# Splitting the experts' up projection into high and low parts, with thinner gathers and six weight places

## The chip, the cores and the metric

One NeuronCore of a Trainium2 chip runs the whole program in one launch. The metric is the device time of that core in microseconds, the median of several runs; a profiled execution gives the trace. Engines: TensorE (PE), VectorE (DVE), ScalarE (ACT), GpSimd (POOL) and SyncE (SP), which only issues transfers.

## The reference, cut to what matters

Two blocks run one after the other on 512 rows of 1024 channels in fp32. The change touches only the last part of the second block, the routed experts:

```python
# 512 tokens, 32 experts, each token goes to 2 experts: 1024 (token, expert) pairs
hf = rmsnorm(x, ffn_norm_g)                     # 512 x 1024
# group top-1 of 4, then top-2 of the 8 experts of that group, gates by softmax
for each expert e, its tokens t (on average 32):
    gt, up = split(hf[t] @ w_gu[e])             # 1024 -> 512, halves of 256
    y = (silu(gt) * up) @ w_down[e]             # 256 -> 1024
    out[t] += gate[t, e] * y
x = x + out
return rmsnorm(x, final_norm_g)
```

Each expert has 2 MB of w_gu and 1 MB of w_down, so 96 MB in all are read once.

## The kernel before, in words

Every engine has its own program, written out by hand (`mo_pe`, `mo_act`, `mo_dve`, `mo_pool`, SyncE's `sp_program`), and named semaphore counts order them: `did(name, key)` counts, `at(name, key)` is what a wait needs. An engine runs its program strictly in the written order.

Before the experts' part come dense layers. They already use a split form: ScalarE copies a weight unit of 128x1024 into WH rounded to fp32r, VectorE writes WL = raw - WH, the activations lie as HH and HL (or R_op, R_ffn), and TensorE adds three fp32r products (high x high, low x high, high x low). In the experts' part of the kernel before, all matmuls are plain fp32.

The experts' part starts with the routing: logits, one-hot choices, ranks, and a matmul that makes for each expert a list of up to 128 places, each with a token number (`mo.idx`), a destination row (`mo.dix`, where an unused place gets a number beyond the last row) and a gate (`mo.gsl`). The normalised rows are stored to DRAM (`hdram`). Line 2388 writes `mo.idx`; an unused place has 0 there, so a gather reads row 0 for it.

Then the loop over 32 experts x (lines 2184 to 2210 for TensorE). POOL gathers 128 rows of 4 KB into one of three places `mo.Xg` and, when done, scatters the results to `ydram` from `mo.Y`. TensorE, in order: the up matmuls of x (8 row tiles, held operand `mo.XT` 128x128, streamed operand 512 weights); 8 transposes of the rows of x+1 (`turned`); the down matmuls of x-1 (`down`, 4 matmuls); for x from 2 to 9 also 4 transposes of the residual; 2 transposes of the hidden rows of x. ScalarE does the sigmoid, half of the copies out of PSUM of the transposed rows, half of the output with the gate, and the hidden rows' copy; VectorE does the products with the sigmoid (two steps of 128x256), the other half of the rows, and the other half of the output. Eight PSUM banks are handed out in a fixed turn (`Turn`).

SyncE loads weights in the order of the list XW: up chunk 0, up chunk 1 of x, down chunk of x-1, 1 MB each, into a ring of nine places (NEXP = 9, `RX`). A place is loaded again when the matmuls that read it nine transfers earlier are done (line 2108). The first nine are issued once the merge before is done; then the rows are stored to DRAM; then the rest.

If an expert has more than 128 rows a guarded part (`ov_...`) handles the rest; it doesn't run in the profile shown.

Of the kernel before, what the change touches and what calls it, by code (L numbers as in the profile page):

```python
# [6 lines left out]
F32 = mybir.dt.float32  # L7
# [9 lines left out]
S = 512  # L17
D = 1024
# [3 lines left out]
NUNIT = 3  # L22
NEXP = 9
NMOE = 20976
BIG = 1.0e30
# [5 lines left out]
for _name, _w in (("ident", 128), ("ones", 128), ("ones64", 128), ("rot64", 128), ("rot32", 128),  # L31
                  ("cd", 128), ("sd", 128), ("tmask", 896), ("causal", 512), ("strict", 128),
                  ("incl64", 64), ("strict64", 64), ("hexp", 128), ("invf64", 1), ("invf32", 1), ("iota", 32), ("io128", 128), ("tok", 4), ("tok2", 4), ("tok3", 4)):
    CO[_name] = (_n, _w)
    _n += _w
# [184 lines left out]
def build(nc, I, out):  # L220
    ctx = ExitStack()
    with ctx:
# [36 lines left out]
        A_sec = phase("second", NA)[0]  # L259
        fast.close()  # L260
        with ExitStack() as st:
            A_moe, RX = sb(st, "A_moe", NMOE), sb(st, "ring_moe", NEXP * SLOT)
# [1794 lines left out]
        NB = 3  # L2057
        ar = Arena(A_moe, 0, 14336)
        mo.htok = t3(ar.take(4 * D), 4)
        mo.Xg = [ar.take(D) for _ in range(NB)]  # L2060
        mo.XT = [t3(ar.take(D), 8) for _ in range(2)]
        mo.sg, mo.hu, mo.hT = ([ar.take(256) for _ in range(2)] for _ in range(3))
        mo.Y = [ar.take(D) for _ in range(NB)]
        ar = Arena(A_moe, 14336, NMOE)
        mo.H = t3(ar.take(8 * S), 8)
# [11 lines left out]
        mo.idx, mo.dix, mo.gsl = ar.take(32).bitcast(U32), ar.take(32).bitcast(U32), ar.take(32)  # L2077
        ov = Mix()
        ov.sel, ov.pos, ov.g, ov.r = ar.take(32), ar.take(4), ar.take(4), ar.take(4)
# [4 lines left out]
        mo.P = [mo.Y[0][:, 0:S], mo.Y[0][:, S:2 * S]]  # L2084
        gu_rows = I["w_gu"].rearrange("e j p n -> (e j p) n")
# [18 lines left out]
        def sp_expert(e, n):  # L2104
            kind, x, j = XW[n]
            if n >= NEXP:
                k0, x0, j0 = XW[n - NEXP]
                e.wait_ge(*at("mo_pe", k0, x0))
            src = I["w_gu"][x, j] if kind == "up" else I["w_dn"][x]
            e.dma(RX[:, n % NEXP * SLOT:(n % NEXP + 1) * SLOT], src).then_inc(*sent(f"x{n % NEXP}", *XW[n]))  # L2110

        MO = tuple(range(8))

        def mo_pe(e):
# [70 lines left out]
            for x in range(32):  # L2185
                b = bank()
                e.wait_ge(*at("mo_act", "xt", x))
                e.wait_ge(*at("mo_dve", "xt", x))
                for j in range(2):
                    w, loaded = xslot("up", x, j)  # L2190
                    e.wait_ge(*loaded)
                    for kt in range(4):
                        t = e.mm(b, mo.XT[x % 2][:, j * 4 + kt, :], w[:, kt * S:(kt + 1) * S], j + kt == 0, j + kt == 4)
                t.then_inc(*did("mo_pe", "up", x))
                if x < 31:
                    turned(x + 1)
# [12 lines left out]
                t.then_inc(*did("mo_pe", "ht", x))  # L2209
# [3 lines left out]
        def mo_act(e):  # L2213
# [25 lines left out]
            turn.next()  # L2239

            def turned(x):
                n, b = turn.next()
                turn.next()
                e.wait_ge(*at("mo_pe", "xt", x, 0))
                if x >= 2:
                    e.wait_ge(*at("mo_pe", "up", x - 2))
                e.act(mo.XT[x % 2][:, 0:4, :], t3(b, 4), ACT.Copy).then_inc(*read("mo_act", turn, n))
                mark("mo_act", "xt", x)

            def down(x):  # L2250
# [8 lines left out]
                mark("mo_act", "y", x)  # L2259

            turned(0)
            for x in range(32):
                n, b = turn.next()
                e.wait_ge(*at("mo_pe", "up", x))
                if x >= 2:
                    e.wait_ge(*at("mo_dve", "hu", x - 2))
                e.act(mo.sg[x % 2], b[:, 0:256], ACT.Sigmoid).then_inc(*did("mo_act", "sg", x))
                if x < 31:
                    turned(x + 1)
                if x:  # L2270
                    down(x - 1)
# [46 lines left out]
        def mo_dve(e):  # L2318
# [43 lines left out]
            for i, (oh, own) in enumerate(((mo.oh1, "tok2"), (mo.oh2, "tok3"))):  # L2362
                e.tt(mo.R[i][:, :, :, 0], oh, bcast(c("tok"), 2, 32), MUL)
                e.tt(mo.R[i][:, :, :, 1], oh, bcast(c(own), 2, 32), MUL)
# [22 lines left out]
            e.wait_ge(*at("mo_pe", "list"))  # L2387
            e.cp(mo.idx, bv[:, :, 0]).then_inc(*did("mo_dve", "idx"))
            e.ts(mo.dix, bv[:, :, 1], 4096.0, None, ADD)
# [12 lines left out]
            step(e.cp(mo.flag, mo.uc[:, 31:32]), "flag")  # L2402

            def turned(x):
                turn.next()
                n, b = turn.next()
                e.wait_ge(*at("mo_pe", "xt", x, 1))
                if x >= 2:
                    e.wait_ge(*at("mo_pe", "up", x - 2))
                e.cp(mo.XT[x % 2][:, 4:8, :], t3(b, 4)).then_inc(*read("mo_dve", turn, n))  # L2410
                mark("mo_dve", "xt", x)

            def down(x):
# [52 lines left out]
        def ov_dve(e0):  # L2466
# [3 lines left out]
            with e0.raw.If(many > 0):  # L2470
# [6 lines left out]
                for j in range(7):  # L2477
# [28 lines left out]
                    for f2 in range(2):  # L2506
                        t = e.cp(mo.XT[0][:, f2 * 4:f2 * 4 + 4, :], t3(bk(f2), 4))
                    t.then_inc(*did("ov_dve", j, "xt"))
# [11 lines left out]
        def ov_pe(e0):  # L2520
            many = over(e0)
            with e0.raw.If(many > 0):
                e = inner(e0)
                for j in range(7):
# [10 lines left out]
                    for kt in range(8):  # L2535
                        t = e.mm(bk(2), mo.XT[0][:, kt, :], RX[:, kt * S:(kt + 1) * S], kt == 0, kt == 7)
                    t.then_inc(*did("ov_pe", j, "gu"))
# [249 lines left out]
def constants():  # L2787
# [41 lines left out]
    put("io128", i[None])  # L2829
    put("tok", i[:, None] + 128 * np.arange(4)[None])  # L2830
    put("tok2", 2 * (i[:, None] + 128 * np.arange(4)[None]) - 4096)
    put("tok3", 2 * (i[:, None] + 128 * np.arange(4)[None]) - 4095)
# [85 lines left out]
```

## Time and profile before

| | us |
|---|---|
| median of 3 runs | 2578.49 (2576.56 to 2578.68) |
| the profiled execution, its own time | 2576.27 |
| its span in the trace | 2574.5 |
| mean granted TensorE clock | 0.934 |
| PE busy | 2380.1 (92%) |
| DVE / ACT / POOL busy | 1150.3 / 757.3 / 192.4 |
| first up matmul of expert 0, last matmul of the loop | 2172.7, 2544.5 |

The page divides the span in 40 slices of 64 us; the digits are tenths of busy time, or of the full clock. The experts' loop takes slices 34 to 39. A group of instructions shows the line of a helper in the code, since each kind of operation has one: L122 matmul, L125 transpose, L129 activation, L135 tensor_tensor, L139 tensor_scalar, L146 copy, L167 transfer, L170 gather, L174 scatter. So groups are told apart by tile. A_moe is the memory of the experts' part, ring_moe the ring of weights. A duration of a matmul in the trace is longer than its step, since matmuls overlap: start to start is the price.

### The profile page before, as it was taken

How to read it: one execution, taken by the hardware profiler on the slowest of the kernel's cores; microseconds unless marked ns; L12 is line 12 of the kernel's file. 1: busy time of each engine (PE TensorE's matmuls, PEld its weight loads, DVE VectorE, ACT ScalarE, POOL GpSimd, SP SyncE). 2: the span in 40 equal slices, each digit the busy share in tenths (PEclk: the TensorE clock that was granted, in tenths of full speed). 3: DMA queues.
4: the chain of work that ended last, by engine and by line, in shares of the span. 5: the costliest groups of instructions: out<-in, count | busy, mean ns of one | idle time of the engine just before them, and what ended most of it. 6: DMA issues, size and time to landing. Idle time of an engine off the chain costs nothing.

```text
span 2574.5 us, 32881 instructions
## 1 busy us (share of the span) xinstructions
PE 2380.1 (92%) x14232; PEld 1722.6 (67%) x14232; DVE 1150.3 (45%) x1771; ACT 757.3 (29%) x1171; POOL 192.4 (7%) x167
## 2 busy tenths in 40 slices
PE   6997799999999987899999998999699998999995
PEld 5884478888888854688888766888344466544442
DVE  6646555435445465555254586333332332111123
ACT  5332543213333324532123332122222122221112
POOL 1112010000001130000000200000000010111110
PEclk9998899999999997999999998999875896999997
DMA  4211012222222110022222221112310043889983
GB/s 159 71 66 49 1 50 98 95 92 93 96 98 68 64 50 17 33 98 98 98 94 92 85 86 59 68 59 72 113 49 1 33 186 128 307 326 340 342 326 145
DMA packets 52420, 283.78 MB, mean 110 GB/s; under 512 B 9136, under 2 KB 9264, under 8 KB 23088
## 3 DMA queue, kind: packets, MB, share of 16 engines
q1 hardware_dynamic: 42048, 257.72, 27.7%
q0 software_dynamic: 9216, 20.99, 2.2%
q8 instruction: 114, 1.87, 0.3%
q10 hardware_dynamic: 1008, 2.92, 0.3%
q14 instruction: 34, 0.28, 0.0%
HBM read 267.44 MB, written 26.74 MB: 114 GB/s over the span
## 4 chain that ended last, share of the span: by engine, by line
PE 84%; DVE 8%; ACT 3%; issue 2%; POOL 1%; DMA 1%; SPq 0%; POOLq 0%; ACTq 0%; DVEq 0%
PE psum L122 81%; PE psum L125 3%; POOL A_mix L135 1%; DVE A_second L135 1%; DVE A_mix L135 1%; ACT A_mix L129 1%; DVE A_second L143 1%; DVE WL L135 1%; DVE A_mix L149 1%; DMA raw<-in_w_in 0%; ACT not_lins L132 0%; DVE A_second L149 0%; DVE A_moe L135 0%; POOL RS L135 0%; ACT HH L129 0%
## 5 line engine op out<-in xcount | busy, mean ns | idle before, releaser
L135 DVE TENSOR_TENSOR WL<-raw,WH 128x1024 fp32r<-128x1024 f32 x236 | 294.8, 1251 | 397.5 <-ACT WH L129 397.4
L129 ACT ACTIVATE WH<-raw 128x1024 fp32r<-128x1024 f32 x236 | 248.4, 1054 | 442.2 <-PE psum L122 431.1
L122 PE MATMUL psum<-ring_moe,A_moe 128*128 128x512 f32 x768 | 343.1, 597 | 1.8 <-DVE A_moe L146 1.1
L122 PE MATMUL psum<-HH,WH 128*128 128x512 f32 x736 | 303.8, 413 | 37.3 <-DVE HL L143 19.2
L122 PE MATMUL psum<-R_op,WH 128*128 128x512 f32 x1024 | 316.1, 390 | 0.0
L122 PE MATMUL psum<-R_ffn,WH 128*128 128x512 f32 x1024 | 315.2, 389 | 0.0
L122 PE MATMUL psum<-HL,WH 128*128 128x512 f32 x736 | 291.2, 396 | 0.0
L122 PE MATMUL psum<-HH,WL 128*128 128x512 f32 x736 | 290.7, 395 | 0.0
L122 PE MATMUL psum<-A_mix 64*128 64x64 f32 (+5 forms) x1984 | 189.1, 328 | 75.4 <-DVE small L161 38.7
L122 PEld LDWEIGHTS psum<-ring_moe,A_moe 128*128 128x128 f32 x768 | 142.1, 192 | 158.0 <-issue 158.0
L122 PE MATMUL psum<-A_second 64*64 64x64 f32 (+3 forms) x3736 | 222.7, 250 | 7.8 <-DVE A_second L135 4.6
L122 PEld LDWEIGHTS psum<-R_op,WH 128*128 128x128 f32 x1024 | 192.2, 188 | 40.8 <-issue 1.0
L122 PEld LDWEIGHTS psum<-R_ffn,WH 128*128 128x128 f32 x1024 | 192.2, 188 | 39.9
L122 PEld LDWEIGHTS psum<-A_mix 64*128 64x128 f32 (+2 forms) x1984 | 132.1, 183 | 117.2 <-DVE small L161 45.4
L122 PEld LDWEIGHTS psum<-A_second 64*64 64x64 f32 (+3 forms) x3736 | 151.8, 144 | 74.3 <-issue 65.5
L122 PE MATMUL psum<-R_op,WL 128*128 128x512 f32 x512 | 199.2, 389 | 0.0
L122 PE MATMUL psum<-R_ffn,WL 128*128 128x512 f32 x512 | 199.2, 389 | 0.0
L122 PEld LDWEIGHTS psum<-HH,WH 128*128 128x128 f32 x736 | 141.0, 192 | 79.3 <-issue 33.5
L122 PEld LDWEIGHTS psum<-HL,WH 128*128 128x128 f32 x736 | 141.2, 192 | 30.1 <-issue 2.9
L122 PEld LDWEIGHTS psum<-HH,WL 128*128 128x128 f32 x736 | 140.8, 191 | 30.7
L129 ACT ACTIVATE A_moe<-psum 128x256 f32<-128x256 f32 (+1 forms) x104 | 47.6, 466 | 265.2 <-PE psum L122 209.4
L135 DVE TENSOR_TENSOR A_moe<-psum,A_moe 128x256 f32<-128x256 f32 (+1 forms) x34 | 14.1, 416 | 224.5 <-ACT A_moe L129 224.5
(191 smaller groups left out, 2691.2 us busy)
## 6 DMA issues: line engine op xcount, KB each, us to landing
ring_moe<-in_w_gu SPq DMA_DIRECT2D x64, 1024.0 KB, 7.1
raw<-in_w_in SPq DMA_DIRECT2D x42, 1024.0 KB, 4.8
raw<-in_w_up SPq DMA_DIRECT2D x32, 1024.0 KB, 4.8
raw<-in_w_down SPq DMA_DIRECT2D x32, 1024.0 KB, 4.8
ring_moe<-in_w_dn SPq DMA_DIRECT2D x32, 1024.0 KB, 7.4
raw<-in_w_out SPq DMA_DIRECT2D x12, 1024.0 KB, 4.8
kept<-A_second SPq DMA_DIRECT2D x22, 256.0 KB, 2.1
A_second<-kept SPq DMA_DIRECT2D x22, 256.0 KB, 5.7
```

Of the source, the lines that this page charges most:

```text
L122: return self.raw.matmul(o, l, r, start=start, stop=stop)
L125: return self.raw.matmul(o, i, ident, is_transpose=True, start=True, stop=True)
L129: return self.raw.activation(o, i, f, scale=scale)
L135: return self.raw.tensor_tensor(o, a, b, op)
L143: return self.raw.scalar_tensor_tensor(o, a, s, b, op0, op1)
L149: return self.raw.reciprocal(o, a)
```

## The change

It does four things. (1) The up matmuls become three fp32r products: new tiles XH, XL (rows) and a ring of four units WH, WL (NSPLIT = 4) of 128x1024, that is a quarter of an expert's w_gu each. ScalarE writes the high parts (`high(u)`), VectorE the low parts (`low(u)`), in their loops where the diff puts them. ScalarE now copies both halves of the turned rows as XH, and VectorE subtracts both as XL. (2) `mo.idx` of an unused place becomes 4096, past the last row, so that the gather leaves it out (its place in Xg keeps what was there; no result of it is used). (3) NEXP 9 becomes 6; a place of an up chunk is free when VectorE has made the low part of its second unit, that of a down chunk when the down matmuls are done. (4) The tiles are laid out anew in the same total memory: XH, XL, WH, WL share what HH, HL, WH, WL of the dense layers used.

```diff
-NEXP = 9
-NMOE = 20976
+NEXP = 6
+NSPLIT = 4
+NMOE = 27120
@@ sp_expert
-                e.wait_ge(*at("mo_pe", k0, x0))
+                e.wait_ge(*(at("mo_dve", "w", 4 * x0 + 2 * j0 + 1) if k0 == "up" else at("mo_pe", "dn", x0)))
@@ mo_pe, loop over x
-                e.wait_ge(*at("mo_act", "xt", x))
                 e.wait_ge(*at("mo_dve", "xt", x))
-                for j in range(2):
-                    w, loaded = xslot("up", x, j)
-                    e.wait_ge(*loaded)
-                    for kt in range(4):
-                        t = e.mm(b, mo.XT[x % 2][:, j * 4 + kt, :], w[:, kt * S:(kt + 1) * S], j + kt == 0, j + kt == 4)
-                t.then_inc(*did("mo_pe", "up", x))
+                for i in range(4):
+                    u = 4 * x + i
+                    e.wait_ge(*at("mo_dve", "w", u))
+                    wh, wl = mo.WH[u % NSPLIT], mo.WL[u % NSPLIT]
+                    for k in range(2):
+                        kt, cs = 2 * i + k, slice(k * S, (k + 1) * S)
+                        xh, xl = mo.XH[x % 2][:, kt, :], mo.XL[x % 2][:, kt, :]
+                        e.mm(b, xh, wh[:, cs], kt == 0, False)
+                        e.mm(b, xl, wh[:, cs], False, False)
+                        t = e.mm(b, xh, wl[:, cs], False, kt == 7)
+                    t.then_inc(*did("mo_pe", "w", u))
+                mark("mo_pe", "up", x)
@@ mo_act
+            def high(u):
+                if u < 128:
+                    w, loaded = split_of(u)
+                    e.wait_ge(*loaded)
+                    if u >= NSPLIT:
+                        e.wait_ge(*at("mo_pe", "w", u - NSPLIT))
+                    e.act(mo.WH[u % NSPLIT], w, ACT.Copy).then_inc(*did("mo_act", "w", u))
@@ mo_act, turned(x)
+                for f2 in range(2):
+                    n, b = turn.next()
+                    e.wait_ge(*at("mo_pe", "xt", x, f2))
+                    if x >= 2:
+                        e.wait_ge(*at("mo_pe", "up", x - 2))
+                    e.act(mo.XH[x % 2][:, 4 * f2:4 * f2 + 4, :], t3(b, 4), ACT.Copy).then_inc(*did("mo_act", "xt", x, f2))
@@ mo_act, loop over x
+            for u in range(4):
+                high(u)
             turned(0)
             for x in range(32):
                 n, b = turn.next()
+                for i in range(3):
+                    high(4 * x + 4 + i)
                 e.wait_ge(*at("mo_pe", "up", x))
                 ... sigmoid
                 if x < 31:
                     turned(x + 1)
+                high(4 * x + 7)
                 if x:
                     down(x - 1)
@@ mo_dve
-            e.cp(mo.idx, bv[:, :, 0]).then_inc(*did("mo_dve", "idx"))
+            e.ts(mo.idx, bv[:, :, 0], 4096.0, None, ADD).then_inc(*did("mo_dve", "idx"))
+            def low(u):
+                if u < 128:
+                    w, _ = split_of(u)
+                    e.wait_ge(*at("mo_act", "w", u))
+                    e.tt(mo.WL[u % NSPLIT], w, mo.WH[u % NSPLIT].bitcast(F32), SUB).then_inc(*did("mo_dve", "w", u))
@@ mo_dve, loop over x
+            for u in range(4):
+                low(u)
             turned(0)
             for x in range(32):
                 n, b = turn.next()
+                for i in range(2):
+                    low(4 * x + 4 + i)
                 e.wait_ge(*at("mo_act", "sg", x))
                 ... two products
                 if x < 31:
                     turned(x + 1)
+                for i in range(2):
+                    low(4 * x + 6 + i)
                 if x:
                     down(x - 1)
```

VectorE's `turned(x)` becomes two subtractions out of PSUM (bank minus XH) in the same manner. The constant `tok4` (token number less 4096) takes the place of `tok` in the lists.

## Rows read from the trace of the kernel before

**Rows 1.** Loop by window: busy us of PE, PEld, DVE, ACT, POOL; clock; DMA share; GB/s.
```profile
2230.00:2502.87 272.87, 272.87 (x827) 134.05 (x826) 51.25 (x93) 50.75 (x100) 48.73 (x48) 1.00 0.90 332
```
**Rows 2.** Order of time in the loop: start us, us, engine, line, operation, count.
```profile
2343.32 1.04 PE L125 MATMUL psum<-C,A_moe 128*128 128x128 f32 x8
2344.19 3.60 PE L122 MATMUL psum<-ring_moe,A_moe 128*128 128x512 f32 x8
2347.63 0.38 PE L125 MATMUL psum<-C,A_moe 128*128 128x128 f32 x2
2347.84 7.03 PE L122 MATMUL psum<-ring_moe,A_moe 128*128 128x512 f32 x16
2354.71 1.04 PE L125 MATMUL psum<-C,A_moe 128*128 128x128 f32 x8
...
2343.93 0.42 DVE L135 TENSOR_TENSOR A_moe<-psum,A_moe 128x256 f32<-128x256 f32 x1 [6.75 <-ACT A_moe L129]
```
**Rows 3.** Order of time, dense fp32r matmuls: alone, then between other work.
```profile
2119.77 0.39 PE L122 MATMUL psum<-HL,WH 128*128 128x512 f32 x1
2120.00 0.19 PEld L122 LDWEIGHTS psum<-HH,WH 128*128 128x128 f32 x1
...
2125.21 0.39 PE L122 MATMUL psum<-HL,WH 128*128 128x512 f32 x1
...
1490.48 0.39 PE L122 MATMUL psum<-HH,WL 128*128 128x512 f32 x1
1490.80 1.99 PE L122 MATMUL psum<-A_second 64*128 64x512 f32 x8
1492.71 0.50 PE L122 MATMUL psum<-HH,WH 128*128 128x512 f32 x1
...
1498.31 0.39 PE L122 MATMUL psum<-HH,WH 128*128 128x512 f32 x1
```
**Rows 4.** Groups (busy us, mean ns, idle before): whole span; loop; feed-forward (last row).
```profile
L135 DVE TENSOR_TENSOR WL<-raw,WH 128x1024 fp32r<-128x1024 f32 x236 | 294.8, 1251 | 397.5 <-ACT WH L129 397.4
L129 ACT ACTIVATE WH<-raw 128x1024 fp32r<-128x1024 f32 x236 | 248.4, 1054 | 442.2 <-PE psum L122 431.1
...
L170 POOL DMA_INDIRECT A_moe<-h_rows,A_moe x24 | 24.5, 1020 | 7.3 <-issue 7.3
L129 ACT ACTIVATE A_moe<-psum 128x256 f32<-128x256 f32 x47 | 18.0, 384 | 170.0 <-PE psum L122 147.5 <-PE psum L125 22.4
L139 DVE TENSOR_SCALAR A_moe<-psum,A_moe 128x512 f32<-128x512 f32 x24 | 18.0, 751 | 57.9 <-PE psum L122 57.9
L129 ACT ACTIVATE A_moe<-psum 128x512 f32<-128x512 f32 x29 | 17.3, 597 | 10.0 <-PE psum L125 8.8
L129 ACT ACTIVATE A_moe<-psum,A_moe 128x512 f32<-128x512 f32 x24 | 16.5, 687 | 37.4 <-PE psum L122 37.4
...
L135 DVE TENSOR_TENSOR relu<-psum,RS 128x512 f32<-128x512 f32 x5 | 3.5, 691 | 6.9 <-PE psum L122 6.9
```
**Rows 5.** Order of time from before the first to the second up.
```profile
2171.42 1.28 ACT L129 ACT_TABLE_LOAD   x1
2172.67 10.02 PE L122 MATMUL psum<-ring_moe,A_moe 128*128 128x512 f32 x16 [1.05 <-DVE A_moe L146]
2184.73 0.67 PE L122 MATMUL psum<-ring_moe,A_moe 128*128 128x512 f32 x1 [0.21 <-issue]
```
**Rows 6.** Landing of the loop's weight loads; the first loads' burst by stage; DMA queue.
```profile
DMA to landing us min/median/max: 4.7/7.2/10.2
2118.00:2123.00 5.00, 5.00 (x24) 4.14 (x23) 0.39 (x1) 1.25 (x2) 1.61 (x2) 1.00 1.01 419
q0 software_dynamic: 9216, 20.99, 2.2%
```
**Rows 7.** Windows, columns as rows 1: attention; start of the experts.
```profile
1950.00:1975.00 25.00, 25.00 (x71) 12.20 (x71) 5.54 (x26) 7.22 (x20) 0.00 (x0) 0.50 0.00 0
2175.00:2180.00 5.00, 5.00 (x9) 1.97 (x8) 0.00 (x0) 0.00 (x0) 0.00 (x0) 0.65 0.15 61
```

More of the change, by code:

```diff
@@ L260, in build @@
         fast.close()
+        with ExitStack() as st:
+            R_moe = sb(st, "R_moe", (4 + 2 * NSPLIT) * D, F32R)
         with ExitStack() as st:
@@ L2057, in build @@
         NB = 3
[L2058 to L2061, printed above, removed]
+        rm = Arena(R_moe, 0, (4 + 2 * NSPLIT) * D)
+        mo.XH, mo.XL = ([t3(rm.take(D), 8) for _ in range(2)] for _ in range(2))
+        mo.WH, mo.WL = ([rm.take(UNIT) for _ in range(NSPLIT)] for _ in range(2))
+        ar = Arena(A_moe, rm.lo, 14336)
         mo.sg, mo.hu, mo.hT = ([ar.take(256) for _ in range(2)] for _ in range(3))
-        mo.Y = [ar.take(D) for _ in range(NB)]
-        ar = Arena(A_moe, 14336, NMOE)
+        ar = Arena(A_moe, 20976, NMOE)
+        mo.htok = t3(A_moe[:, 20976:20976 + 4 * D], 4)
+        mo.Xg, mo.Y = ([ar.take(D) for _ in range(NB)] for _ in range(2))
+        ar = Arena(A_moe, 14336, 20976)
         mo.H = t3(ar.take(8 * S), 8)
@@ L2078, in build @@
         ov = Mix()
+        ov.XT = t3(mo.Xg[1], 8)
         ov.sel, ov.pos, ov.g, ov.r = ar.take(32), ar.take(4), ar.take(4), ar.take(4)
@@ L2083, in build @@
         mo.ss, mo.rr = ar.take(4), ar.take(4)
-        mo.P = [mo.Y[0][:, 0:S], mo.Y[0][:, S:2 * S]]
+        mo.P = [mo.Y[1][:, 0:S], mo.Y[1][:, S:2 * S]]
         gu_rows = I["w_gu"].rearrange("e j p n -> (e j p) n")
@@ L2107, in sp_expert, with split_of @@
                 k0, x0, j0 = XW[n - NEXP]
-                e.wait_ge(*at("mo_pe", k0, x0))
+                e.wait_ge(*(at("mo_dve", "w", 4 * x0 + 2 * j0 + 1) if k0 == "up" else at("mo_pe", "dn", x0)))
             src = I["w_gu"][x, j] if kind == "up" else I["w_dn"][x]
             e.dma(RX[:, n % NEXP * SLOT:(n % NEXP + 1) * SLOT], src).then_inc(*sent(f"x{n % NEXP}", *XW[n]))
+        def split_of(u):
+            w, loaded = xslot("up", u // 4, u % 4 // 2)
+            return w[:, u % 2 * UNIT:(u % 2 + 1) * UNIT], loaded
         MO = tuple(range(8))
@@ L2239, in mo_act @@
             turn.next()
-            def turned(x):
[L2242 to L2248, printed above, removed]
+            def high(u):
[5 more added lines that the diff above has]
+                    e.act(mo.WH[u % NSPLIT], w, ACT.Copy).then_inc(*did("mo_act", "w", u))
+            def turned(x):
+                for f2 in range(2):
[4 more added lines that the diff above has]
+                    e.act(mo.XH[x % 2][:, 4 * f2:4 * f2 + 4, :], t3(b, 4), ACT.Copy).then_inc(*did("mo_act", "xt", x, f2))
             def down(x):
@@ L2362, in mo_dve @@
             for i, (oh, own) in enumerate(((mo.oh1, "tok2"), (mo.oh2, "tok3"))):
-                e.tt(mo.R[i][:, :, :, 0], oh, bcast(c("tok"), 2, 32), MUL)
+                e.tt(mo.R[i][:, :, :, 0], oh, bcast(c("tok4"), 2, 32), MUL)
                 e.tt(mo.R[i][:, :, :, 1], oh, bcast(c(own), 2, 32), MUL)
@@ L2402, in mo_dve @@
             step(e.cp(mo.flag, mo.uc[:, 31:32]), "flag")
-            def turned(x):
[L2405 to L2410, printed above, removed]
+            def low(u):
[3 more added lines that the diff above has]
+                    e.tt(mo.WL[u % NSPLIT], w, mo.WH[u % NSPLIT].bitcast(F32), SUB).then_inc(*did("mo_dve", "w", u))
+            def turned(x):
+                for f2 in range(2):
+                    n, b = turn.next()
+                    e.wait_ge(*at("mo_act", "xt", x, f2))
+                    e.tt(mo.XL[x % 2][:, 4 * f2:4 * f2 + 4, :], t3(b, 4), mo.XH[x % 2][:, 4 * f2:4 * f2 + 4, :].bitcast(F32),
+                         SUB).then_inc(*read("mo_dve", turn, n))
                 mark("mo_dve", "xt", x)
@@ L2506, in ov_dve @@
                     for f2 in range(2):
-                        t = e.cp(mo.XT[0][:, f2 * 4:f2 * 4 + 4, :], t3(bk(f2), 4))
+                        t = e.cp(ov.XT[:, f2 * 4:f2 * 4 + 4, :], t3(bk(f2), 4))
                     t.then_inc(*did("ov_dve", j, "xt"))
@@ L2535, in ov_pe @@
                     for kt in range(8):
-                        t = e.mm(bk(2), mo.XT[0][:, kt, :], RX[:, kt * S:(kt + 1) * S], kt == 0, kt == 7)
+                        t = e.mm(bk(2), ov.XT[:, kt, :], RX[:, kt * S:(kt + 1) * S], kt == 0, kt == 7)
                     t.then_inc(*did("ov_pe", j, "gu"))
@@ L2830, in constants @@
     put("tok", i[:, None] + 128 * np.arange(4)[None])
+    put("tok4", i[:, None] + 128 * np.arange(4)[None] - 4096)
     put("tok2", 2 * (i[:, None] + 128 * np.arange(4)[None]) - 4096)
```

2 lines of the change are left out of this document (1 added, 1 removed).

## Prediction

> **What bounds the kernel now.** I read the page's table of 40 slices first: from about 2170 us to the end TensorE, the clock and the DMA are all high at once, and only this stretch, the experts' loop, is changed. The busy times by stage come next [rows 1]: over 273 us TensorE is busy for the whole window at full clock (1.00 is the 2.4 GHz level), with the DMA at 0.90 of its time, VectorE at 51 us and ScalarE at 51 us. So TensorE has no gap to give back; only less TensorE work can shorten the loop, until another resource is late. The order of time on TensorE [rows 2] gives one expert: 8 transposes of gathered rows 2343.32 to 2344.19 (0.87), 4 down matmuls in 8 halves to 2347.63 (3.44), 2 transposes of the hidden rows to 2347.84 (0.21), 8 up matmuls in 16 halves to 2354.71 (6.87). Period: 2354.71 - 2343.32 = **11.39 us**. An fp32 matmul here runs as two halves of 0.43 us each.
>
> **The up matmuls.** Removed: 8 fp32 matmuls, 6.87 us per expert. Added: 24 in fp32r (three products for each of 8 row tiles). Their shape, 128x128 held and 128x512 streamed, is that of the dense layers. [rows 3] bracket their price: from 2119.77 to 2125.21 lie 24 steps, 5.44 us, so 0.227 each where nothing but fp32r runs; the 24 steps from 1492.71 to 1498.31, just after other work, take 5.60, and leaving fp32r takes 0.32 instead of 0.23 (1490.48 to 1490.80), 0.09 more. The new loop has both seams in each expert, so I take the second: 5.60 + 0.09 = 5.69, saving 1.18; the other end is 5.44, saving 1.43. New period **10.21** (9.96 without seams). Held operands are now rows and streamed ones weights, the other way round than in those rows; the shapes are the same, so I price this swap at nothing, and the rival "no overlap of loads" covers its failure.
>
> **The splitting, beside TensorE.** Per expert ScalarE gets 4 copies of 128x1024 (1.05 each) and one more 128x512 copy (0.60); VectorE gets 4 subtractions of 128x1024 (1.25) and two of 128x512 from PSUM (0.69) in place of one copy [rows 4]. Whole load: ScalarE 4x1.05 + 2x0.60 + 0.38 + 0.69 + 0.38 = 6.85; VectorE 4x1.25 + 2x0.69 + 2x0.42 [rows 2] + 0.75 = 7.97. Both are under 10.21, but order decides. I lay one period out, t = 0 at the first up matmul of expert x. The first product with the sigmoid starts 0.61 us after the next transposes begin, 0.38 of it the sigmoid [rows 2, 4]; I give 0.2 of the rest to the hand-over from TensorE and 0.03 to that between the others. A place of WH is free after each six matmuls, at 1.40, 2.80, 4.20. ScalarE: high parts of the next expert's units at 1.45, 2.85 and 4.25 to 5.3, sigmoid 5.9 to 6.3, XH 6.35 to 7.55, last high part to 8.6, output half 8.6 to 9.3, hidden copy at 10.4. VectorE: low parts 2.5 to 3.75 and 3.9 to 5.15, hidden rows 6.3 to 7.2, XL 7.2 to 8.6, low parts to 11.1, output half to 11.85. TensorE: transposes 5.69 to 6.56, down 6.56 to 10.0, next up at 10.21. It wants XL, ready at 8.6 (slack 1.6); its third low part at 13.0, ready at 9.85 (slack 3.1). The added waits thus find their events long past. What is queued behind them: behind ScalarE's wait for a WH place the sigmoid (0.6 us of room); behind VectorE's wait for the sigmoid the XL parts and the last two low parts. PSUM places are re-used after eight turns, six or seven of them in one period, as before. If this cover is gone, every us past 1.6 in the chain up, sigmoid, hidden rows, XL is paid in full, 31 times.
>
> **Six weight places.** A weight place is now freed by VectorE's low part and not by the last up matmul; but SyncE issues in order, so the next two up chunks stand behind the wait of a down chunk, which is free at -0.2. Issues: down and first up chunk at -0.2, second up chunk at 0.9 (after the low part that ends at 11.1 of the period before). Wanted: first up chunk at 11.7, second at 14.5, down chunk at 16.8; so they have 11.8, 13.6 and 17.0 us. Landings in the loop took 4.7 to 10.2, median 7.2 [rows 6]. Fewer places therefore cost nothing, with 1.6 us left above the longest landing.
>
> **Gathers.** A gather brings 128 rows of 4 KB (0.52 MB); the 32 scatters together write the 1024 valid ones (4.2 of the 21.0 MB of the software queue [rows 6]), so 32 gathers move 16.8 MB and would move 4.2. Per expert 3.15 + 0.52 + 0.13 = 3.80 MB becomes 3.41. On a critical path that is worth nothing while TensorE paces; it pays for the faster loop. The loop's 332 GB/s at a share of 0.90 means 369 GB/s, so 9.2 us per expert; the burst of first loads ran at 419 GB/s [rows 6], so 8.1. Both are below 10.21. POOL's 1.02 us for each gather [rows 4] I leave, though it could shrink with the rows; POOL waits most of the loop anyway (49 of 273 us busy, [rows 1]).
>
> By the Trainium skill (SBUF — State Buffer, "A bandwidth-pool intuition that's wrong"), a core gets about 358 GB/s from HBM; the burst row is above that, so the trace disagrees. By that figure the transfers would need 9.5 us per expert, and the sum would be the same with 0.7 us of room.
>
> The new subtractions read two SBUF operands while POOL writes descriptors. No row shows the two together in the loop; bounds are 0 and the whole 1.02 us twice per expert on VectorE: 7.97 + 2.03 = 10.0, still under 10.21, and a gather issued two experts ahead has over 10 us. I take 0.
>
> The Trainium skill (SBUF — State Buffer, "SBUF: two separate sides") has VectorE instructions with two SBUF inputs and GpSimd instructions that read SBUF exclude one another for their whole length; that speaks against this change, and the bound just given holds what it could cost.
>
> **Start and end.** Before: the first rows are turned at half clock, the first up starts at 2172.67 and takes 9.86 us since the clock is 0.50, and 0.65 on average from 2175 to 2180: full for the last 0.3 of these 5 us, so from 2178.5; the second starts at 2184.73 [rows 5, 7]. After: four low parts (5 us) go ahead of the first row parts on VectorE, behind the routing, whose last steps run while the gather is under way. I take them as hidden behind the gather: XL starts at 2171.7 (the first XH is there by 2171.4, where the table load starts) and ends at 2173.1, so +0.4; if nothing hid them, it would be up to +5. Half clock until 2178.5 does 5.4/0.454 = 12 matmuls, the other 12 end near 2181.3. But ScalarE's table load for the sigmoid (1.28 us, now hidden at 2171.42) will come behind the third high part, 2181.0 to 2182.3; so sigmoid 2182.7, hidden rows 2183.6, XL 2185.0. The second up starts at 2185.0 rather than 2184.7: **+0.3 us**. Bounds 0 to +8: the four low parts unhidden, or half clock through the whole first expert (3 us more). The end (last down, reload of results, norm) has no changed step.
>
> **Sum.** 31 x 1.18 = 36.6, less 0.3 = 36.3 us. The profiled execution took 2576.3 us, 1.8 more than its 2574.5 span and 2.2 less than the median of 2578.5; the span should become 2538.2, and the median **2542.2 us**. Without seams: 31 x 1.43 - 0.3 = 44.0, or 2534.5.
>
> **Rivals.**
> A, TensorE paces (my forecast), period 9.96 to 10.5: 2534 to 2551. For it: all slack above. Chance 0.77.
> B, hand-overs or landings are late by some tenths up to 1 us per expert: the SyncE issues come in a burst of three, so landings could rise over 11.8 us, or the XL chain could be 2 us longer than laid out. At 0.7 us per expert: 2542 + 31x0.7 = 2564 (range 2551 to 2573). For: landings of 10.2 already with nine places. Against: less traffic. Chance 0.14.
> C, no overlap of weight loads with the stream: 0.19 (load) + 0.23 (step, [rows 3]) = 0.42 per matmul, 24 are 10.1 us, 3.2 more than now; the place is the up part, it decides from 0.286 per matmul (6.87/24), and the time is 2578.5 + 31x3.2 = 2678, slower. Against: in [rows 3] each load starts with the previous matmul. Chance 0.02.
> D, the clock stays low. [rows 7] has a stretch in which TensorE is busy for all 25 us and the clock is still 0.50, and the new start has two gaps of over 1 us. Each expert at half clock costs 10.2 more; it decides at 3.6 experts, and through the whole loop it gives 2542 + 31x10.2 = 2858, slower. Against: dense fp32r windows stand at 1.00 throughout [rows 3], and so did the loop's fp32 [rows 1]. Chance 0.03.
> E, the edit saves matmul time but the waits give just that much back (within 5 us of 2578.5): 0.04.
> The Trainium skill (TensorE: Matmul & The Clock Gate, "HAM oscillation") has thin tiles of 128 rows drop to the low clock when TensorE waits for loads between them; it would add to D, with D's time, and the loop's row at 1.00 speaks against it.
>
> **How the numbers follow.** Range: A in full and B up to 2558: 2533 to 2558, which leaves out half of B and C, D, E, and a little of A's fast side: some 0.18. A change of 0.2% is 5.2 us, about what can be told here. Faster: A and B, 0.91, plus the small-stall side of E and D, 0.01: 0.92; same 0.04; slower 0.04.
>
> **What would show it.** Period on TensorE of 10.2 with no idle between transposes and up; 24 matmuls in 5.4 to 5.7; clock 1.00 from the second expert; DMA share about 0.80 to 0.90 at 330 to 340 GB/s; XL ending 1.5 us before the next up; software queue 8.4 MB. Idle on TensorE released by VectorE's XL or WL would show B; a weight load not under the matmul before it, C; PEclk under 1 after 2190 us, D.

## The result

The changed kernel takes **2533.9 us** (median of 4 runs, 2533.3 to 2537.0) against 2577.5 of the kernel before on the same chips: 43.6 us less, ratio 0.983 (95% interval 0.982 to 0.985). The forecast was 2542.2 within 2533 to 2558. The span of the profiled execution is 2531.1 us against 2574.5.

The loop by window, columns as in [rows 1]: TensorE is still busy for the whole window at full clock; VectorE's share went from 0.19 to 0.74, ScalarE's from 0.19 to 0.67, and the DMA moves about as many GB/s as before, with fewer bytes per expert in a shorter period.

```profile
2230.00:2470.00 240.00, 240.00 (x1019) 168.84 (x1018) 176.50 (x215) 160.56 (x220) 62.32 (x47) 1.00 0.88 338
```

TensorE's order of time in the loop of the changed kernel, which answers to [rows 2]:

```profile
2333.35 1.04 PE L126 MATMUL psum<-C,A_moe 128*128 128x128 f32 x8
2334.22 3.60 PE L123 MATMUL psum<-ring_moe,A_moe 128*128 128x512 f32 x8
2337.66 0.38 PE L126 MATMUL psum<-C,A_moe 128*128 128x128 f32 x2
2337.80 5.73 PE L123 MATMUL psum<-R_moe 128*128 128x512 f32 x24
2343.36 1.04 PE L126 MATMUL psum<-C,A_moe 128*128 128x128 f32 x8
```

From start to start: rows' transposes 0.87, down part 3.44, hidden rows' transposes 0.14 (0.21 before), up part 5.56 (6.87 before). Period 2343.36 - 2333.35 = **10.01 us** against 11.39: 1.38 less, for two reasons of 1.31 and 0.07.

What runs beside it, in the same period (order of time; the number in brackets is the idle time before, with its releaser):

```profile
2333.55 0.38 ACT L130 ACTIVATE A_moe<-psum 128x256 f32<-128x256 f32 x1 [0.25 <-PE psum L123]
2333.99 1.08 ACT L130 ACTIVATE R_moe<-psum 128x512 fp32r<-128x512 f32 x2
2334.76 1.28 DVE L136 TENSOR_TENSOR R_moe<-psum,R_moe 128x512 fp32r<-128x512 f32 x2
2335.96 2.35 DVE L136 TENSOR_TENSOR R_moe<-ring_moe,R_moe 128x1024 fp32r<-128x1024 f32 x2
...
2340.63 2.53 DVE L136 TENSOR_TENSOR R_moe<-ring_moe,R_moe 128x1024 fp32r<-128x1024 f32 x2 [1.65 <-ACT R_moe L130]
2341.15 1.60 POOL L171 DMA_INDIRECT A_moe<-h_rows,A_moe  x1 [0.30 <-issue]
```

XL ends at 2334.76 + 1.28 = 2336.04, and the next up part starts at 2337.80: 1.76 us of slack. The gather on GpSimd takes 1.60 here, and 1.02 in [rows 4].

The time that weight loads of the loop take from issue to landing (min, median, max us), which answers to [rows 6], and the software queue on the page:

```profile
DMA to landing us min/median/max: 4.7/8.0/13.2
...
DMA packets 52424, 271.26 MB, mean 107 GB/s; under 512 B 12208, under 2 KB 12336, under 8 KB 23088
q0 software_dynamic: 9216, 8.42, 1.0%
```

The start of the experts' part, answering to [rows 5]; TensorE, and the table load on ScalarE:

```profile
2167.26 1.97 PE L126 MATMUL psum<-C,A_moe 128*128 128x128 f32 x8 [4.50 <-DMA A_moe<-h_rows,A_moe]
2171.44 7.54 PE L123 MATMUL psum<-R_moe 128*128 128x512 f32 x24 [2.21 <-DVE R_moe L136]
2178.80 1.28 ACT L130 ACT_TABLE_LOAD   x1
2178.82 1.04 PE L126 MATMUL psum<-C,A_moe 128*128 128x128 f32 x8
2181.44 0.44 PE L126 MATMUL psum<-C,A_moe 128*128 128x128 f32 x2 [1.58 <-DVE A_moe L136]
2182.64 7.11 PE L123 MATMUL psum<-R_moe 128*128 128x512 f32 x24 [0.76 <-DVE R_moe L136]
```

**Where the 43.4 us of span went.** The second expert's up part starts 2.1 us earlier (2184.73 to 2182.64); from there to the start of the last expert's up part the kernel before needs 345.5 us and the changed one 305.4 (2182.64 to 2488.00), 40.1 less; from there to the last down part 11.25 and 9.93, 1.3 less; the end is equal within 0.1. The 40.1 are 30 periods of 1.38 less 1.3 us for the second expert, whose up part took 6.95 us because the clock was not yet full. Of the 2.1 us at the start 1.8 lie ahead of the first changed step of TensorE, ScalarE or VectorE: the transposes of the normalised rows start at 2147.62 against 2149.39. From there to the issue of the first gather 0.6 is lost (2163.93 against 2165.12), while TensorE makes the lists at a lower clock (3.70 us against 3.11). From that issue to the first rows' transposes 1.2 is won (3.33 us against 4.53), and from these to the second up part 0.3 is lost.

### The profile page after: what moved, and what is told of

Read it like the earlier page. It is cut to its first block, busy times and chain, and to the rows that moved or that the text cites. A ratio compares the mean times of both kernels' runs of the same rounds, so it can differ in the third digit from the quotient of the medians.

```text
span 2531.1 us, 33743 instructions
## 1 busy us (share of the span) xinstructions
PE 2336.0 (92%) x14488; PEld 1770.0 (70%) x14488; DVE 1317.5 (52%) x1931; ACT 904.2 (36%) x1331; POOL 212.6 (8%) x167
## 2 busy tenths in 40 slices
DMA packets 52424, 271.26 MB, mean 107 GB/s; under 512 B 12208, under 2 KB 12336, under 8 KB 23088
## 3 DMA queue, kind: packets, MB, share of 16 engines
q0 software_dynamic: 9216, 8.42, 1.0%
## 4 chain that ended last, share of the span: by engine, by line
PE 84%; DVE 8%; ACT 3%; issue 2%; POOL 1%; DMA 1%; SPq 0%; ACTq 0%; POOLq 0%; DVEq 0%
PE psum L123 81%; PE psum L126 3%; POOL A_mix L136 1%; DVE A_second L136 1%; DVE A_mix L136 1%; ACT A_mix L130 1%; DVE A_second L144 1%; DVE WL L136 1%; DVE A_mix L150 1%; ACT not_lins L133 0%; DMA raw<-in_w_in 0%; DVE A_moe L136 0%; DVE A_second L150 0%; POOL RS L136 0%; ACT HH L130 0%
## 5 line engine op out<-in xcount | busy, mean ns | idle before, releaser
L123 PE MATMUL psum<-R_moe 128*128 128x512 f32 x768 | 186.7, 400 | 3.0 <-DVE R_moe L136 3.0
L136 DVE TENSOR_TENSOR R_moe<-ring_moe,R_moe 128x1024 fp32r<-128x1024 f32 x128 | 153.5, 1221 | 60.8 <-ACT R_moe L130 58.3
L123 PEld LDWEIGHTS psum<-R_moe 128*128 128x128 f32 x768 | 144.3, 191 | 32.9 <-issue 2.6
L130 ACT ACTIVATE R_moe<-ring_moe 128x1024 fp32r<-128x1024 f32 x128 | 135.5, 1062 | 55.7 <-PE psum L123 55.7
```

What stands on the lines that cost most here:

```text
L123: return self.raw.matmul(o, l, r, start=start, stop=stop)
L130: return self.raw.activation(o, i, f, scale=scale)
L136: return self.raw.tensor_tensor(o, a, b, op)
```

## The experiments

The theory: TensorE paces both loops; the gain is its matmul time and nothing else; six places and thin gathers are only room. The rivals are that the gain, or part of it, is relief of the transfers; or that the new work beside TensorE already costs something. Medians are held against the kernel before on the same chip (2575.6 to 2576.2), as ratios with their 95% interval; "above the changed kernel" means above its 2534 to 2535 us.

**Full gathers in the changed kernel.**

```diff
-                e.tt(mo.R[i][:, :, :, 0], oh, bcast(c("tok4"), 2, 32), MUL)
+                e.tt(mo.R[i][:, :, :, 0], oh, bcast(c("tok"), 2, 32), MUL)
-            e.ts(mo.idx, bv[:, :, 0], 4096.0, None, ADD).then_inc(*did("mo_dve", "idx"))
+            e.cp(mo.idx, bv[:, :, 0]).then_inc(*did("mo_dve", "idx"))
```

> The changed kernel with the full gathers back: an unused place reads row 0 again, 0.52 MB per expert and not 0.13. Theory (TensorE paces, 10.01 us per expert in the changed kernel's trace): the transfers need 3.80 MB per expert; at the burst's 419 GB/s that is 9.1 us, so nothing is lost: within 3 us of the changed kernel's 2534. Rival (the transfers would pace without the thin gathers): at 369 GB/s, the rate that the old loop implies, it is 10.3 us, 0.3 us per expert over TensorE's 10.01, so 2534 + 31 x 0.3 = 2543; if it is worse, idle time of TensorE before the first up matmul or before the splits shows it. A gather takes 1.72 us on GpSimd in the changed kernel and took 1.02 before: if the 1.72 stays here, the new VectorE work and not the left-out places lengthens it.

Measured: 2533.9 us, ratio 0.984 (0.983 to 0.986), so nothing lost. The same window of the loop:

```profile
2230.00:2470.00 240.00, 240.00 (x1019) 168.61 (x1018) 175.90 (x215) 160.52 (x220) 62.54 (x47) 1.00 0.97 377
```

The DMA stands at 0.97 of its time with 377 GB/s and TensorE still doesn't wait. The rate implied by [rows 1], 369 at a full share, was too low as a limit. So the thin gathers gave nothing of the 43.6 us that can be told from the noise, though they keep the DMA further from its limit. What they do change is the first landing. In the ten profiles with thin gathers the first rows' transposes start 3.2 to 3.5 us after the start of the first gather's instruction, and in the four with full ones 4.4 to 4.6. In the changed kernel XL then waits for the low parts, so that only 0.5 us of this reaches the first up part (7.51 us after that start, 8.04 with full gathers).

**Thin gathers alone in the kernel before** (the reverse edit).

> The kernel before with one part of the change alone: gathers leave out the unused places. Theory: TensorE paces at 11.39 us per expert with or without it, so no difference: 2577 within 2 us, and the DMA's busy share in the loop falls from 0.90 to about 0.80 (3.41 MB per 11.39 us, 300 GB/s). Rival (the gain came from relieved transfers): a good part of the 43.6 us appears here. A gather on GpSimd: 1.02 us if the VectorE splits are what lengthens it to 1.72, 1.7 if the left-out places do.

Measured: 2574.2 us, ratio 1.000 (0.999 to 1.001). Share 0.83 and 299 GB/s. The gathers on GpSimd in this kernel (min, median, max ns, count), their landing, and the same two lines of the changed kernel with full gathers:

```profile
L170 POOL DMA_INDIRECT A_moe<-h_rows,A_moe x25: 1017/1017/1024, 2199.6 to 2476.6; - x25
DMA to landing us min/median/max: 4.5/5.6/6.9
```

```profile
L171 POOL DMA_INDIRECT A_moe<-h_rows,A_moe x27: 1512/1591/2027, 2206.7 to 2470.7; - x27
DMA to landing us min/median/max: 8.8/10.0/12.2
```

Left-out places don't lengthen a gather's instruction (1.02 us in the first fence). In the changed kernel it takes 1.5 to 2.0 us, with full gathers too, and the traces show when: if it starts while VectorE runs a subtraction of two SBUF operands, it ends 2.12 us after that subtraction began, as if it waited for its end and then took its 1.02. In the changed kernel it starts 0.52 us into one and takes 1.60 (2340.63 and 2341.15 above), or 0.10 into one and takes 2.02. In the run with five places below it starts 0.34 into one and takes 1.78; the next gather there starts 0.23 us ahead of the subtraction and takes 1.02. One that starts with a subtraction (2165.44 and 2165.43 in the changed kernel) takes 1.00 as well. The two of the run with five places:

```profile
2335.67 1.78 POOL L171 DMA_INDIRECT A_moe<-h_rows,A_moe  x1 [0.30 <-issue]
2345.64 1.02 POOL L171 DMA_INDIRECT A_moe<-h_rows,A_moe  x1 [0.30 <-issue]
```

By the Trainium skill (SBUF — State Buffer, "SBUF: two separate sides") such an instruction and a GpSimd one that reads SBUF exclude each other, and whichever starts first keeps the other waiting for the whole instruction. These durations agree on the side of GpSimd alone: VectorE's subtractions take 1.22 us in the loop and 1.25 in the dense layers [rows 4], and the pair that starts behind the gather at 2345.64 takes 2.36 us, as pairs do elsewhere in that run.

**Six places alone in the kernel before.**

```diff
-NEXP = 9
+NEXP = 6
```

> The kernel before with six weight places in place of nine, nothing else. Theory: a load is still issued a whole period ahead, so nothing changes: 2577 within 2 us. An up chunk is issued when the up matmuls of two experts earlier end, and wanted 4.5 us plus one up part less than two periods later, over 11 us; landings took up to 10.2. Rival: with six places the fp32 loop waits for loads, by up to 1 us per expert, 2577 to 2608, and the shorter hold of a place by the splits is what makes six enough.

Measured: 2575.4 us, ratio 1.000 (0.999 to 1.001); landings 4.7 to 10.3, median 7.7. Fewer places cost nothing there.

**Half a dose: one chunk of two split.** The second chunk of each expert runs as four fp32 matmuls from rows copied in fp32; only half of the high and low parts are made.

```diff
-                for i in range(4):
+                for i in range(2):
...
+                w, loaded = xslot("up", x, 1)
+                e.wait_ge(*loaded)
+                for kt in range(4):
+                    t = e.mm(b, mo.XT[x % 2][:, kt, :], w[:, kt * S:(kt + 1) * S], False, kt == 3)
```

> The changed kernel with the split for one of the two up chunks of each expert alone; the other runs as four plain fp32 matmuls, as before. A half dose: if TensorE's matmul time is all of the gain, the up part takes 12 x 0.227 + 8 x 0.43 + 0.1 = 6.2 us in place of 5.56 (changed) and 6.87 (before), the period is 10.7, and the time lies in the middle: 2534 + 31 x 0.66 = 2554. Rival (the price is in changes between fp32r and fp32 work, 0.1 to 0.3 us each, which this version has once more): up to 6.5 us for the up part, 2563. Rival (the gain is of another kind, such as less traffic, which stays whole here): 2534.

Measured: 2551.7 us, ratio 0.991 (0.989 to 0.992). The period:

```profile
2340.00 1.04 PE L126 MATMUL psum<-C,A_moe 128*128 128x128 f32 x8
2340.87 3.60 PE L123 MATMUL psum<-ring_moe,A_moe 128*128 128x512 f32 x8
2344.30 0.38 PE L126 MATMUL psum<-C,A_moe 128*128 128x128 f32 x2
2344.44 3.02 PE L123 MATMUL psum<-R_moe 128*128 128x512 f32 x12
2347.30 3.59 PE L123 MATMUL psum<-ring_moe,A_moe 128*128 128x512 f32 x8
2350.73 1.04 PE L126 MATMUL psum<-C,A_moe 128*128 128x128 f32 x8
```

10.73 us, between 11.39 and 10.01, with 12 fp32r steps in 2.86 and 8 halves in 3.43. The full dose saved 1.38 per expert, the half 0.66: the loop's gain is the matmul time, and it grows in proportion. (The whole run saves more than half, 24.5 of 40.8 us on this chip, because its start is shorter too: from the first rows' transposes to the second up part its profile has 12.6 us, where the changed kernel has 15.4 and 15.9.) The price of a change between the two kinds is small: 2.86 - 12 x 0.227 = 0.14.

**2.3 us put into the chain to XL.** Four needless copies follow the sigmoid.

```diff
                 e.act(mo.sg[x % 2], b[:, 0:256], ACT.Sigmoid).then_inc(*did("mo_act", "sg", x))
+                if x < 31:
+                    for i in range(4):
+                        e.act(mo.scr, Xt[:, 0, :], ACT.Copy).then_inc(*did("mo_act", "dup", x, i))
+                        e.wait_ge(*last("mo_act"))
```

> The changed kernel with four needless copies of 128x512 on ScalarE right behind the sigmoid, per expert but the last, each waited for: about 4 x 0.64 = 2.6 us put into the chain up part, sigmoid, XH, XL, next up part. In the changed kernel's trace XL ends at 2336.04 and the next up part starts at 2337.80: slack 1.76. Theory (the chain has that slack and beyond it each us is paid in full): 2.6 - 1.8 = 0.8 us per expert, 31 x 0.8 = +25 us, 2559, with TensorE idle before the up part released by VectorE's XL. Rival 1 (the chain already paces): +2.6 per expert, 2614. Rival 2 (slack wider than it looks): no change, 2534.

Measured: 2555.2 us, ratio 0.992 (0.991 to 0.994), 21 us above the changed kernel. The wait that is new:

```profile
2337.68 1.29 DVE L136 TENSOR_TENSOR R_moe<-psum,R_moe 128x512 fp32r<-128x512 f32 x2 [2.25 <-ACT R_moe L130]
2338.25 0.38 PE L126 MATMUL psum<-C,A_moe 128*128 128x128 f32 x2
2339.03 5.77 PE L123 MATMUL psum<-R_moe 128*128 128x512 f32 x24 [0.40 <-DVE R_moe L136]
```

XL ends at 2338.97 and the up part starts 0.06 later. The period is 10.69 (transposes of the hidden rows at 2338.25 and 2348.94), 0.68 over 10.01; 31 x 0.68 = 21. XL came 2.3 us later after the sigmoid, of which 1.7 was slack. So the chain has the slack that the trace showed, and past it the time is paid in full.

**Two more subtractions on VectorE.**

```diff
+                    for i in range(1):
+                        e.tt(t3(mo.scr, 4), t3(b, 4), mo.XH[x % 2][:, 4 * f2:4 * f2 + 4, :].bitcast(F32), SUB).then_inc(*did("mo_dve", "dup", x, f2, i))
+                        e.wait_ge(*last("mo_dve"))
                     e.tt(mo.XL[x % 2][:, 4 * f2:4 * f2 + 4, :], ...
```

> The changed kernel with two needless subtractions of 128x512 out of PSUM on VectorE, one ahead of each XL part, each waited for: 2 x 0.74 = 1.5 us more work on VectorE in each expert and 1.5 us later XL. Theory: the slack of 1.76 covers the chain, and VectorE's own work of 7.6 + 1.5 = 9.1 us stays under the 10.01 us period, so 2534 within 3 us. Rival (VectorE, once its waits for ScalarE's high parts are counted, is as long as the period): up to +1.5 per expert, 2580.

Measured: 2536.1 us, ratio 0.985 (0.984 to 0.987). The loop's period stays 10.01 (up parts at 2340.95 and 2350.96); some 1.5 us come before each of the first two up parts, where XL is on the path (TensorE idle for 3.65 and 2.21 us there, in place of 2.21 and 0.76). VectorE is then busy 208 of 240 us and still doesn't pace.

**Five places.**

```diff
-NEXP = 6
+NEXP = 5
```

> The changed kernel with five weight places in place of six. It measures how much room the ring has. With six, loads are issued in a burst of three when a down chunk's place comes free (2337.86 to 2339.1 in the trace) and take up to 13.2 us (median 8.0); an up chunk is wanted about 11.5 us after its issue. With five a place is asked for again five transfers later: the first up chunk of x+2 waits for the second up chunk of x (its low part ends at the end of the period), the second for the down part before it, the down chunk for the first up chunk. Theory: each load is issued a third of a period later (3.3 us), so with 8 us to land and about 8 us left it comes in about on time: between 0 and 1 us lost per expert, 2534 to 2565, with idle time released by ring_moe's loads. Rival (six is already at the edge, as landings of 13 us suggest): over 2 us per expert, above 2596.

Measured: 2537.2 us, ratio 0.985 (0.983 to 0.986), 2 to 3 us above the changed kernel, which isn't clear of the noise since the intervals overlap; TensorE is busy 239.2 of 240 us. Now loads are late for their first reader:

```profile
ACT R_moe L130 <- DMA ring_moe<-in_w_gu: 42.8, 36, 3.5
```

42.8 us of ScalarE's time in 36 waits, the longest 3.5, nearly all of it taken up by the slack of the splits. So with five the loads begin to be late, and six has room.

**Without the third product.** It is left out of the computation.

```diff
                         e.mm(b, xh, wh[:, cs], kt == 0, False)
-                        e.mm(b, xl, wh[:, cs], False, False)
-                        t = e.mm(b, xh, wl[:, cs], False, kt == 7)
+                        t = e.mm(b, xl, wh[:, cs], False, kt == 7)
```

> The changed kernel without the third product (high rows x low weights), which is left out of the computation: 8 matmuls fewer per expert, all else as it is, the splits included. It asks what is late next behind TensorE. TensorE alone: 10.01 - 8 x 0.227 = 8.2 us per expert, 31 x 1.8 = 56 us less, 2478. VectorE's own work is 4 x 1.22 + 2 x 0.68 + 2 x 0.42 + 0.74 = 7.8 us and ScalarE's 6.9, both near it. Transfers: 3.41 MB need 8.1 us at 419 GB/s, 9.2 us at 369. Theory: the transfers or the order of VectorE's work take over at about 9.0 us per expert: 2534 - 31 x 1.0 = 2503, with idle time on TensorE. Rival (all cover is wide): 2478. By the Trainium skill (SBUF - State Buffer, 'A bandwidth-pool intuition that's wrong') HBM gives about 358 GB/s, so 9.5 us and 2518.

Measured: 2507.8 us, ratio 0.974 (0.973 to 0.976): 26 us less than the changed kernel, not 56. TensorE, busy 219.6 of 240 us, now waits, and for rows rather than for weights:

```profile
PE psum L126 <- DMA A_moe<-h_rows,A_moe: 21.8, 15, 2.9
PEld psum L126 <- DMA A_moe<-h_rows,A_moe: 29.2, 18, 3.3
ACT R_moe L130 <- DMA ring_moe<-in_w_gu: 33.4, 35, 2.0
```

The first two rows are one wait, seen by the matmuls and by the weight loads ahead of them, so TensorE lost 21.8 us to it; the 51 us in the next expectation add the two.

**The same with full gathers.**

> The changed kernel without the third product (left out of the computation) and with the full gathers back, to be held against the version without the third product alone (2508). There TensorE waited 51 us for gathered rows in the loop. Theory (transfers are next behind TensorE, and only there do thin gathers pay): 3.80 MB per expert at the 377 GB/s that the changed kernel with full gathers sustained is 10.1 us per expert against about 9.1 with thin gathers, so 31 x 1.0 = +31 us, 2539. Rival (the waits come from when a gather is issued, not from how much it brings): within 5 us of 2508.

Measured: 2518.4 us, ratio 0.978 (0.976 to 0.979), 11 us above the run before it; expected were 31 or under 5, so neither. Its loop:

```profile
2230.00:2470.00 240.00, 213.26 (x858) 140.02 (x857) 182.06 (x222) 157.14 (x226) 62.81 (x49) 0.98 0.98 392
```

The transfers ran at 392 GB/s, over the 377 on which the 31 rested; at 392, 3.80 MB are 9.7 us. So the thin gathers pay in the loop only once TensorE no longer paces. How much of the remaining wait comes from when a gather is issued (behind the scatter on GpSimd) wasn't tried.

**A better start.** This run makes three edits to the changed kernel at once. Four of the eight groups of residual transposes go into TensorE's wait for the first gather, a small sigmoid loads the table early, and the first XL comes ahead of the third low part.

```diff
+            e.act(mo.sg[0][:, 0:4], rcol, ACT.Sigmoid).then_inc(*did("mo_act", "tab"))
+            for i in range(NEARLY):
+                k, f2 = divmod(i, 2)
+                ... copy of the residual, as in the loop
             turned(0)
...
-            for u in range(4):
+            for u in range(2):
                 low(u)
             turned(0)
+            for u in range(2, 4):
+                low(u)
```

> A version that should beat both: the changed kernel with (a) four of the eight groups of residual transposes put into TensorE's wait for the first gather (4.5 us idle there), (b) the sigmoid's table load done by a small sigmoid before, and (c) the first row parts XL ahead of the third and fourth low part. By the trace: (a) 4 x 0.43 = 1.7 us less in the loop, hidden before it; (b) the wait before the hidden rows' transposes in the first expert falls from 1.58 by up to 1.3 us; (c) the first up part starts 0.8 us earlier. Sum 3.8 us, and up to 3 more if TensorE's clock, 0.50 until about 2177.5 and 0.72 on average from 2180 to 2185, is full through the second expert: 2527 to 2530. Rival (the start is set by something else, as the first gather, and the loop by what is common): 2532 to 2534.

Measured: 2528.0 us, ratio 0.982 (0.980 to 0.983). The start:

```profile
2164.22 3.15 PE L127 MATMUL psum<-C,X 128*128 128x128 f32 x16
2169.03 1.09 PE L127 MATMUL psum<-C,A_moe 128*128 128x128 f32 x8 [1.66 <-DMA A_moe<-h_rows,A_moe]
2171.78 5.74 PE L124 MATMUL psum<-R_moe 128*128 128x512 f32 x24 [1.66 <-DVE R_moe L137]
2180.20 5.70 PE L124 MATMUL psum<-R_moe 128*128 128x512 f32 x24 [0.79 <-DVE R_moe L137]
```

From the first rows' transposes to the second up part 11.2 us in place of 15.4. The clock was full when the gather landed (0.50 in the changed kernel), and the first two up parts take 5.58 and 5.54 us. The table load now leaves 0.61 us of idle time before the hidden rows' transposes (1.58 before), and the first up part waits 1.66 us for XL (2.21 before). What each of the three edits is worth by itself was not measured.

**All eight groups early.**

> As the version with four early groups of residual transposes, but with all eight groups ahead of the first gather's landing. In that version TensorE still waited 1.66 us for the gather, the clock was full from the first expert on, and a group costs 0.8 us at half clock or 0.43 at full. Four more groups cost 1.7 to 3.1 us before the first expert, 0 to 1.5 of it over the remaining wait, and take 1.7 us out of the loop: 2526.5 to 2528. Rival (PSUM banks and ScalarE's copies, 8 x 0.6 us, hold up the first rows): 2530 or more.

Measured: 2526.4 us (2524.5 to 2529.7), ratio 0.981 (0.980 to 0.982), the best of all and the same as with four within the intervals. The first up part ran partly at the lower clock in its profile (7.1 us).

**The changed kernel once more.**

> The changed kernel itself, on the same chip as the other runs of this call. It is to come out at 2534 (ratio 0.983 to the kernel before); its trace gives a second start of the experts' part: theory, the start moves by 1 to 3 us from run to run with the moment at which TensorE's clock falls, and the loop's period is 10.01 in both.

Measured: 2535.4 us, ratio 0.984 (0.983 to 0.986); period 10.01. The transposes of the normalised rows start at 2151.31 (2147.62 in the first profile), and from the rows' transposes to the second up part it is 15.9 us.

## Why the prediction was right, point by point

**What bounds it.** Right: TensorE paces before and after. The half dose and the two single edits of the old kernel show that the loop's gain is its matmul time and nothing else that was changed.

**The up part.** Mechanism right, size off, and this is the term that was mis-sized. I took 5.69 (fp32r between other work in [rows 3], 5.60, and 0.09 for leaving it); measured was 5.56, and the hidden rows' transposes before it shrank from 0.21 to 0.14. Entering and leaving fp32r thus cost 5.56 - 5.44 = 0.12, less the 0.07 gained in front: 0.05 net, against the 0.25 that I had priced. 0.20 x 31 = 6.2 us of the 7.3 by which the forecast saving (36.3) missed the 43.6. For the period the low end of the bracket was the nearer (9.96 against 10.01 measured and 10.21 forecast), though the up part itself came out midway. That the low end's 2534.5 is so close to the 2533.9 is partly luck: it has 1.6 us too much in the loop and leaves out the 1.3 that the second expert lost at the lower clock, against a start that came 2.4 us better than it assumed. The rows at 1492.71 had other work of another shape before them, and I let the word "seam" outweigh 24 clean steps.

**The start.** I gave +0.3 us. From the first rows' transposes to the second up part the kernel before needs 15.08 us and the changed one 15.38: +0.3. That the two agree is luck, since its parts were other than laid out: the first XL waited for the four low parts (2.21 us idle before the first up part), which I had taken as hidden, since the thin gather landed 1.2 us sooner than the full one; the clock rose earlier, and the table load cost what was expected (1.58 idle in place of 0.52). In the second profile it was +0.8. The remaining 1.1 us of the miss is a second up part that started 2.1 us earlier where I had it 0.3 later, less the 1.3 us that the second expert lost at the lower clock. Most of the 2.1 are the 1.8 us ahead of the transposes of the normalised rows. In all fourteen profiles of this document that point lies between 2147.2 and 2152.1 us, at 2147.6 and 2151.3 in the two of the changed kernel alone, so it moves from run to run and isn't the change's. Held against the kernel before on its chip the repeat saved 40.8 us (2576.2 to 2535.4), so 2 to 3 us of the 43.6 are no more than what moves from run to run.

**Work beside TensorE.** Right. Slack of the XL chain 1.6 laid out, 1.76 in the trace, 1.7 by the experiment on ScalarE; VectorE has room for 1.5 us more.

**Six places.** Right in the time, by a thinner margin than claimed: landings rose to 13.2 us where 10.2 had been the longest, while I allowed 11.8 for the first up chunk. Yet no wait of ScalarE for a load shows in the loop. Both landings of 13.2 us (issued at 2215.4 and 2225.9) are second up chunks, for which I had allowed 13.6; the first up chunks took 7.2 to 10.4. So the room that I gave as 1.6 us was 1.4 for the first chunk and some 0.4 for the second. With five places the waits come, and the splits' slack takes up nearly all of them.

**Gathers.** Right for the loop, where they are worth nothing while TensorE paces. The traffic limit that I worked out from a share of 0.90 (369 GB/s) was wrong: 377 and 392 GB/s were sustained. By the Trainium skill the 358 GB/s of one of its pages is a core's share when both cores of a pair stream, and a core alone reaches about 425 (HBM Reference, "Specifications (TRN2)"); these runs agree with that and not with 358 as a limit of this kernel, which the prediction had beside it. That a gather would keep its 1.02 us was wrong (1.72 on average): I had bounded what the new subtractions could cost on VectorE's side, where nothing was lost, and the 0.7 us came on GpSimd's, off the path. The sooner first landing I had left out.

**Rivals.** C (no overlap of loads) would have shown 10.1 us in the up part, D a clock under 1.00 in the loop; both fell. B (late hand-overs or landings) showed only in the kernels made to show it, and E (waits that give the gain back) not at all.

## What to carry to other kernels

Where one engine is busy for whole windows, price a change by the start-to-start steps of that engine alone, and use what runs beside it only to ask which wait ends last; here the period was TensorE's sum in both kernels and at half the dose. Relief of a resource that isn't late (thin gathers, a deeper ring) measures as nothing until the bound moves, and then it is worth a part of what bytes over rate would say. And when steps in a steady run and steps after a switch differ, test the switch's price with shapes as near to the new ones as the trace has, before letting it into the sum.

## What the runs showed of the hardware

- fp32r as three products is cheaper than fp32: 24 steps of 0.227 us (5.56 with entry and exit) against 16 halves of 0.43 (6.87), for held tiles of 128x128 and streamed ones of 128x512.
- A gather that leaves out three of four places still sends as many packets (9216 on the software queue in both kernels); the bytes fall from 20.99 to 8.42 MB, and the packets under 512 B rise from 9136 to 12208, by just the 3072 places left out.
- A gather's instruction on GpSimd takes 1.02 us, and more when it starts within a VectorE subtraction of two SBUF operands: it then ends 2.12 us after that subtraction began (0.10 into it 2.02 us, 0.34 into it 1.78, 0.52 into it 1.60). One that starts with the subtraction or 0.23 us ahead of it takes 1.00 to 1.02. VectorE's own durations don't change.
- The median landing of a thin gather goes from 5.6 us in the old kernel to 8.6 in the changed one although it brings the same rows. The longer instruction is at most 1.0 us of this; the cause of the rest was not separated.
- The DMA sustained 392 GB/s over 240 us, with weights, gathers and scatters mixed.
- The granted clock was 0.50 from 2160 us on and still 0.50 when the first gathered rows came, after 4.5 us of idle TensorE. With 16 transposes put into that wait it was 0.50 from 2160 to 2165 too, and 1.00 from 2167 to 2169, when the rows came.
